# A half chunk's sum split around a gate's addition, and a turned half copied ahead of a square

## The reference

```python
ada = silu(cvec) @ w_ada + b_ada                     # shift, scale, gate, twice
h = rmsnorm(x, norm_mix) * (1 + sc1) + sh1
p = h @ w_in                                         # four mixers: pooling, long conv, short conv, attention
gates = sigmoid(h @ w_gate + b_gate)                 # 4 x 1024 columns
merged = ga*(ya @ w_br_a) + gb*(yb @ w_br_b) + gc*(yc @ w_br_c) + gd*(yd @ w_br_d)
x = x + g1 * (merged @ w_out)
h2 = rmsnorm(x, norm_ffn) * (1 + sc2) + sh2
x = x + g2 * moe(h2)                                 # 4 groups of 8 experts, top 1 group, top 2 experts
y = rmsnorm(x, norm_final)
```

## Time and profile before

| what | value |
|---|---|
| median of 3 runs | 1067.54 us (1066.78 to 1068.22) |
| profiled execution, its own time | 1062.43 us |
| its span | 1060.8 us |
| TensorE busy | 997.9 us, 94% of the span |
| VectorE busy | 568.6 us, 54% |
| ScalarE busy | 229.2 us, 22% |
| GpSimd busy | 206.7 us, 19% |
| mean granted TensorE clock | 0.987 |
| DMA | 210.89 MB, mean 199 GB/s |

### The profile page before, as it was taken

The page is one execution under the profiler, slowest core; times in us unless marked ns, Lnnn a source line. Parts: engine busy times, 40 slices in busy tenths (PEclk is TensorE's granted clock), DMA queues, the critical chain, the costliest instruction groups (busy, mean ns, idle before and its releaser), DMA issues.

```text
span 1060.8 us, 13977 instructions
## 1 busy us (share of the span) xinstructions
PE 997.9 (94%) x5099; PEld 604.1 (57%) x5099; DVE 568.6 (54%) x1318; ACT 229.2 (22%) x453; POOL 206.7 (19%) x270
## 2 busy tenths in 40 slices
PE   4999999999999999999999999999989999986976
PEld 2567776877655555666666666554556555443532
DVE  4577758144687678777768434245564333212237
ACT  4120001000354454444421100021121111100103
POOL 2340000010593001011121421112121333321200
PEclk9999999999999999999999999999999999988999
DMA  9952211250543343232222741571899999999994
GB/s 321 291 157 65 80 40 40 74 159 6 179 138 118 113 138 115 80 120 80 80 80 79 254 152 40 197 160 40 312 380 388 415 414 415 413 415 414 414 406 172
DMA packets 94053, 210.89 MB, mean 199 GB/s; under 512 B 7791, under 2 KB 63661, under 8 KB 85665
## 3 DMA queue, kind: packets, MB, share of 16 engines
q1 hardware_dynamic: 81952, 184.96, 48.2%
q0 software_dynamic: 11792, 24.93, 6.9%
q10 hardware_dynamic: 240, 0.11, 0.0%
HBM read 201.16 MB, written 20.40 MB: 209 GB/s over the span
## 4 chain that ended last, share of the span: by engine, by line
PE 70%; SPq 10%; DVE 10%; DMA 6%; issue 3%; ACT 2%; DVEq 0%; ACTq 0%; POOLq 0%
PE pair L2145 24%; PE pair L2138 10%; PE pair L2190 7%; SPq L789 4%; SPq L803 4%; PE pair L2521 4%; PE pair L2326 3%; PE pair L2137 3%; PE pair L2141 3%; PE pair L2410 3%; DVE hyena_region L1718 2%; DVE ring_region L1718 2%; DMA mixer_region<-in_w_e_down 2%; PE pair L2538 2%; PE pair L2359 1%
## 5 line engine op out<-in xcount | busy, mean ns | idle before, releaser
L2138 PE MATMUL pair<-hT_region,ring_region 128*128 128x512 f32 x192 | 98.3, 594 | 0.0
L1016 POOL TENSOR_TENSOR dft_region<-dft_region,padded_region 128x640 f32<-128x640 f32 x24 | 38.4, 1600 | 299.6 <-DVE padded_region L1640 299.6
L2145 PE MATMUL pair<-hT_region,ring_region 128*128 128x320 f32 x336 | 94.8, 435 | 0.1
L2145 PEld LDWEIGHTS pair<-hT_region,ring_region 128*128 128x128 f32 x336 | 63.0, 190 | 29.2 <-issue 3.9
L2019 DVE TENSOR_TENSOR mixer_region<-pair,mixer_region 128x128 f32<-128x128 f32 x32 | 9.3, 291 | 124.6 <-ACT mixer_region L1302 122.6
L2190 PE MATMUL pair<-ring_region,dft_region 128*128 128x512 f32 x160 | 73.1, 607 | 2.4 <-issue 2.3
L2137 PEld LDWEIGHTS pair<-hT_region,ring_region 128*128 128x128 f32 x192 | 35.4, 190 | 46.2 <-issue 42.7
L1718 DVE SCALAR_TENSOR_TENSOR ring_region<-ring_region,scT 128x256 f32<-128x256 f32 x112 | 56.1, 501 | 0.0
L1718 DVE SCALAR_TENSOR_TENSOR hyena_region<-ring_region,scT,hyena_region 128x256 f32<-128x256 f32 x112 | 56.0, 500 | 0.0
L1032 POOL DMA_INDIRECT mixer_region<-h_rows,token_rows x32 | 32.8, 1024 | 117.4 <-PE pair L2141 87.2
L1302 ACT ACTIVATE mixer_region<-pair 128x128 f32<-128x128 f32 x32 | 8.9, 277 | 193.9 <-PE pair L2521 135.3
(11 more groups left out here) (501 smaller groups left out, 1939.4 us busy)
## 6 DMA issues: line engine op xcount, KB each, us to landing
ring_region<-in_w_ada SPq DMA_DIRECT2D x24, 1024.0 KB, 8.1
ring_region<-in_w_gate SPq DMA_DIRECT2D x16, 1024.0 KB, 5.6
ring_region<-in_w_in SPq DMA_DIRECT2D x13, 1024.0 KB, 5.6
ring_region<-in_w_e_gate SPq DMA_DIRECT2D x11, 1024.0 KB, 18.5
ring_region<-in_w_e_up SPq DMA_DIRECT2D x11, 1024.0 KB, 22.6
ring_region<-in_w_e_down SPq DMA_DIRECT2D x20, 512.0 KB, 21.4
hyena_region<-in_w_e_gate SPq DMA_DIRECT2D x10, 1024.0 KB
hyena_region<-in_w_e_up SPq DMA_DIRECT2D x10, 1024.0 KB
```

Of the source, the lines that this page charges most:

```text
L1016: pool.tensor_tensor(merged[:, dj, :], merged[:, dj, :], gtmp, ALU.add).then_inc(merged_add, 1)
L2138: return mm(ps_[0:m, W0 + TC:1024], lhsT, rhs[:, TC:T], start=start, stop=stop)
L2145: ins = mm(out, weights[:, kt, :], columns[:, kt, :], start=(kt == 0), stop=(kt == KD // 2 - 1))
```

## The change

VectorE: sum_half takes a range of rows. At the five n it is called for rows 0 and 1 (4 instructions) ahead of mix_gates and for rows 2 to 7 (12 instructions) behind it. ScalarE: the square and square root of a tile's second half are issued behind the copy of ("ha", t) and no longer at ("ob", t) ahead of it. TensorE, GpSimd and the DMA queues have the same program.

```diff
-                elif k == "ob":
-                    t = st[1]
-                    act.wait_ge(x1_done, 2 * t + 2)
-                    own.link(act.activation(apart_halves[0], x1[:, t, HD2:D], ACT.Square, accum_out=ssq[:, t:t + 1]))
-                    act.activation(rms[:, t:t + 1], ssq[:, t:t + 1], ACT.Sqrt, bias=ssq_part[:, t:t + 1], scale=1.0 / D
-                                   ).then_inc(ssq2_done, 1)
                 elif k in ("ha", "hb"):
...
                     frees(act.activation(hturned[t % 2][:, k0:k0 + 4, :],
                                          ps(st)[:, 0:HD2].rearrange("p (k t) -> p k t", k=4), ACT.Copy), st)
+                    if k == "ha":
+                        act.wait_ge(x1_done, 2 * t + 2)
+                        own.link(act.activation(apart_halves[0], x1[:, t, HD2:D], ACT.Square, accum_out=ssq[:, t:t + 1]))
+                        act.activation(rms[:, t:t + 1], ssq[:, t:t + 1], ACT.Sqrt, bias=ssq_part[:, t:t + 1], scale=1.0 / D
+                                       ).then_inc(ssq2_done, 1)
...
-            def sum_half(c, h):
+            def sum_half(c, h, rows=range(KD)):
...
-                computed(dve, PLACE["ada", c, h][2])
-                if c > 4:
-                    computed(dve, ("part", c - 1, h))
+                if rows[0] == 0:
+                    computed(dve, PLACE["ada", c, h][2])
+                    if c > 4:
+                        computed(dve, ("part", c - 1, h))
+                else:
+                    own.wait()
                 sums = [apart[:, h, :], w[:, 0, :]]
-                for kt in range(KD):
+                for kt in rows:
...
                 own.wait()
-                dve.sem_inc(ada_summed, 1)
+                if rows[-1] == KD - 1:
+                    dve.sem_inc(ada_summed, 1)
...
                     if k == "gp" and n in HALVES and not alone(n):
-                        sum_half(*HALVES[n])
+                        sum_half(*HALVES[n], range(0, 2))
                     mix_gates(st)
+                    if k == "gp" and n in HALVES and not alone(n):
+                        sum_half(*HALVES[n], range(2, KD))
```

## The result

The changed kernel takes 1059.29 us (median of 6 runs, 1058.13 to 1062.48), the kernel before beside it 1066.29 (median of 6, 1064.56 to 1068.22). The ratio is 0.9938, 95% interval 0.9923 to 0.9954: 6.6 us faster, between 4.9 and 8.2. The forecast was a gain of 4.27 us to 1063.3, range 1060.0 to 1067.0. In the table of the experiments, e6's median is that of five runs: its sixth took 1166.77 us, a tenth longer than the others, and is left out. The profiled execution takes 1060.90 us, its span is 1059.3.

The account below looks back on a forecast made before the run. TensorE bounds most of the kernel, the expert weight stream the last quarter. Gains of 2.25 us (splits) and 3.95 (copy), 6.20 together, less 1.93 for the clock, leave 4.27: from 1067.54 to 1063.3 us, range 1060.0 to 1067.0.

Parts of the forecast that it names:

- the four splits: Sum split around the gate's addition at n = 12, 14, 16, 18: TensorE gains 0.92, 0.92, 0.76, 0.92, together 3.52 us.
- the clock at n = 10: TensorE's clock falls behind its 1.78 us stand before the scores at n = 10, costing 1.93 us; taken as likelier.
- n = 10: Split there leaves VectorE idle for ScalarE's copy; TensorE stands 1.78 us before the scores and loses 1.27 us.
- part 2: ScalarE's copy of (ha, t) ahead of the square: wins 3.95 us at tile 2, gap and clock.
- Tile 2: In (hb, 2) the 2.02 us gap goes, and the low clock behind it, 1.93 us over eight matmuls.
- the early choice: VectorE's early choice of experts, next to be late, ends 737.71 us, wanted at 737.97: fits with 0.26 us to spare.
- Rival C: Timed runs of before have no clock fall at tile 2: gain 4.27 or 2.34 us, 1063.3 to 1065.2; chance 0.20.
- Tile 4: Copy comes earlier and (route, 4) could start 0.35 us sooner; counted as nothing, bounds 0 and 0.35 us.
- Pass-through to the end: What TensorE wins before about 745 us moves the whole expert weight stream forward and reaches the end in full.
- rival D: Win lost downstream because the DMA stream alone sets the end; time stays at 1067.5 us; chance 0.12.
- Rival E: VectorE held before the gate's addition at all five n: slower, 1069.9 us, or 1071.9 with a clock fall; chance 0.07.
- rival B: No fall of the clock at n = 10: the full gain of 6.20 us, to 1061.3 us; chance 0.25.

Follow-up runs that it names:

- e6: Whole change, but the sum at n = 10 left unsplit, measured a second time: 1057.16 us, ratio 0.9929 against the kernel before.
- e7: Kernel before with three filler matmuls put into TensorE's 2.02 us gap in (hb, 2) at tile 2: 1063.11 us, ratio 0.9984.
- e10: Kernel before with the sum split at n = 12, 14, 16 and 18 alone, ScalarE's order as before: 1060.21 us, ratio 0.9953.
- e9: Kernel before with the sum split at n = 10 alone, ScalarE's order as before: 1067.56 us, ratio 1.0022.
- e1: The kernel before, unchanged, measured again for noise and a second profile: 1065.91 us, ratio 0.9991.
- e8: Changed kernel with two filler matmuls in the gap before the scores of n = 10: 1059.03 us, ratio 0.9939 against the kernel before.
- e3: Kernel before with only ScalarE's copy of (ha, t) moved ahead of the square, sums unsplit: 1062.68 us, ratio 0.9967.
- e4: Whole change, but the sum at n = 10 left unsplit, first measurement: 1056.74 us, ratio 0.9906 against the kernel before.
- e12: Whole change with n = 10 unsplit, plus two fillers ahead of the counts and the numbers: 1056.76 us, ratio 0.9918 against the kernel before.
- e2: Kernel before with only VectorE's sums split at all five n, ScalarE's order as before: 1064.88 us, ratio 0.9990.

## Why the prediction was right or wrong

**The step that failed: two terms of the sum and its start.** The term of the four splits was put at 3.52 us; the profiles show 4.02, and timed runs more. The start of the sum, 1067.54 us, was the median of three runs and 1.25 us above the 1066.29 of the comparison. The other term, the 1.93 us taken off for the clock at n = 10, came out lower in the timed comparisons within a group (1.1 to 1.4 us), but no run settles its size. The next paragraphs take these in turn.

**The four splits (3.52 us): right in mechanism, the term too small.** The wait on the gate's addition went, and the later addition of "gm" (L1679) is late next, as forecast. The limit was the end of that addition, which I moved by 0.30 us; it moved by 0.06. From the profiles of e7 (unsplit) and e6 (split), which stand at the same place at n = 10 (scores at 425.87 and 425.82), ("O", n) starts at 451.80, 478.28, 503.51 and 530.36 in the one and 450.59, 476.12, 500.57 and 526.29 in the other. Less the 0.05 they began apart, the gains are 1.16, 0.95, 0.78 and 1.13 us, together 4.02. TensorE still waits for L1679 at all four places (0.31, 0.19, 0.19 and 0.31 us in e6), so that addition is the limit everywhere: 0.92 us and the 0.30 - 0.06 = 0.24 us that the split costs less, 1.16 us, at n = 12 and, within 0.03, at 18. At n = 14 and 16 it ends later, because VectorE stands for ScalarE's copy ahead of the gate's addition. In e6's timeline:

```profile
469.46 0.49 DVE L1675 TENSOR_TENSOR padded_region<-pair,mixer_region 128x320 f32<-128x320 f32 x1 [0.26 <-ACT mixer_region L1255]
...
493.92 0.49 DVE L1675 TENSOR_TENSOR padded_region<-pair,mixer_region 128x320 f32<-128x320 f32 x1 [0.44 <-ACT mixer_region L1255]
```

Less the 0.06 us that stands there without the copy, this is 0.20 and 0.38 us, and 1.16 - 0.20 = 0.96 and 1.16 - 0.38 = 0.78 are the two gains. I had such a hold at n = 16 alone, with 0.16 us. The list of waits fell by less than 4.02, by 4.3 - 1.0 = 3.3 us: at n = 12 the branch's product starts 0.65 us behind the start of the turning matmuls in e6 and 2.10 in e7, 1.45 us apart, 0.17 more than the wait of 1.28. A wait that goes can win a little more than its entry in the list. e10 timed gives 5.0 (3.5 to 6.4), which holds 4.02 and, barely, 3.52.

**n = 10: the gap right, the clock priced as certain from one profile.** That VectorE would idle for the copy, that TensorE would lose 1.27 us and stand 1.78 us, was right. That the clock would fall was right for five profiles of five; where it fell it cost 3.1 us in two of them and 1.6 in three, 2.2 in the mean. Timed, the clock is left with 1.1 us in e9 (-0.3 to 2.4). A least-squares fit of three additive terms to the ten comparisons of the changed kernel and its parts (e1, e7 and e8 left out) gives, as an estimate, 4.6 us for the four splits (3.7 to 5.6), 2.7 us lost at n = 10 (1.8 to 3.5) and 3.9 us for part 2 (3.0 to 4.8); the intervals are rough, because the runs of before are shared. By it the clock at n = 10 costs 2.7 - 1.27 = 1.4 us (0.5 to 2.2). So a cost of the clock there is shown, and that it is less than 1.93 is likely and not shown. How often the clock falls at n = 10 in executions that weren't profiled, no run here shows, and whether a fall removed there comes back later stays open too. In each of the fourteen profiles the clock falls at some point between 775 and 798 us, in the five without the fall of n = 10 and without a gap at tile 2 (e3, e4, e6, e8, e12) before 779 us, in the other nine, e7 with its filled gap among them, at 781.9 us or later. But from the start of the last sixteen projection matmuls to the end of the first expert's first group those five take 38.0 us in the mean (36.7 to 39.2) and the other nine 37.7 (36.6 to 39.2), so no repayment can be read from it.

**Tile 2 (2.02 + 1.93 us): right, the clock's part a little too large.** Gap and low clock went, the early choice (VectorE's last step ends at 738.46, TensorE wants it at 738.94) was in time with 0.48 us to spare. The prediction compared the eight slow matmuls with the next eight (3.44 us) and not with the same eight at full clock (3.67 us, as in e10 behind the gap), so the profile gives 3.72 us and not 3.95. e3 gives 3.5 us (2.1 to 4.8), e7 gives 1.7 for the clock alone. The gap brought the fall in four of five profiles (before, e1, e2, e9; not e10), so the mean price is below 1.70. Rival C, a fall that is luck of the profiled execution, is refuted as a rule by e7, and true of one profile in five.
The Trainium skill, "TensorE: Matmul & The Clock Gate", section "The HAM clock gate", has the point where the clock changes vary from run to run. Here the same gap at n = 10 was followed by a fall that cost 3.1 us in two profiles and 1.6 in three, and the gap of tile 2 by none in e10; that agrees.

**Tile 4: nothing, right**, and for the reason given.

**Pass-through to the end: right, rival D refuted.** In the profiles of before and after the first load is 2.97 us earlier, but the first expert's first group ends at 797.92 before and 796.36 after, 1.56 us earlier, because the clock falls at 791 us after and the group takes 4.98 us in place of 3.67; the spans differ by 1.5. In e12 the group starts 794.25 - 787.24 = 7.0 us earlier, and the span is 1060.8 - 1053.9 = 6.9 shorter. The profiled run of before was a cheap one (1062.43 us where the medians are 1065 to 1066), so 1.5 us isn't the gain.

**Rival E, slower: refuted** outside n = 10. There its mechanism is just what happens, and e9, which is that mechanism alone, is the slowest kernel of the study.

**The sum.** With the sizes shown, 4.02 - 1.27 - 1.1 + 3.5 to 3.72 = 5.2 to 5.4 us; measured 5.6, 6.0 and 6.6. The rest is within the intervals. Parts measured alone add up to 5.0 - 2.3 + 3.5 = 6.2 us, or, with e2 in place of e9 and e10, to 1.1 + 3.5 = 4.6; the noise allows both. That the first is the 6.20 of rival B is chance: B had no cost of the clock at n = 10 and too small a term for the splits. Of the 4.0 us between 1063.3 and 1059.29, 1.25 us is the high start: with 1066.29 in its place the forecast would have been 1062.0 and the time inside the range moved with it. The other 2.7 us is a gain of 7.0 us between the medians where 4.27 was forecast: 0.5 us of it is the splits by the profiles (1.1 by the fit), 0.5 to 0.8 the price of n = 10, and the rest can't be told from noise.

## What to carry to other kernels

An in-order engine that sums ahead of a short operation which others wait for should do that one first, but only where its input is there: split at the place where the input arrives, count each place by itself, and leave out the one that has to wait. Here four of five places give 4 to 5 us, the fifth takes 2 to 3 back, and leaving it out is the better kernel. A gap of TensorE can cost nearly as much again in clock (1.7 us behind 2.02); price that by filling the gap with idle work in a kernel of its own, with enough runs, and not from one profile.

## What the runs showed of the hardware that was not expected

- The clock fell behind the gap of 1.8 us at n = 10 in 5 of 5 profiles, behind the one of 2.02 us at tile 2 in 4 of 5, and never at either place when matmuls filled it (1 of 1 each) or the gap was gone. Waits of 1.28 us in front of the branch's product had no fall behind them.
- The low clock lasts unequally long from execution to execution: in e4, e8 and e9 it held from 776 to 786, 777 to 787 and 786 to 797 us, in before from 784 to 788; e3 has two falls, at 777 and at 784 us.
- VectorE stands 0.21 us at the end of a sum where it waits for its own last write and then signals, but only 0.06 us at n = 12 where it waits for that write and doesn't signal.
